# First feed-forward block of an encoder layer: shift rows loaded last, raw first results finished with a bias, and the opening's order set by the scheduler

## What is computed

```python
cc = jax.nn.silu(c)
mod = (cc @ w_ada[l] + b_ada[l]).reshape(b, N_ADA, D_MODEL)
sh1, sc1, gt1, sh2, sc2, gt2, sh3, sc3, gt3 = [mod[:, i, None, :] for i in range(N_ADA)]
h = modulate(rms_norm(x, g_ffn1[l]), sh1, sc1)          # h * (1 + scale) + shift
x = x + 0.5 * gt1 * swiglu(h, w_ffn1_in[l], w_ffn1_out[l])   # a, b = split(h @ w_in); (silu(a) * b) @ w_out
h = modulate(rms_norm(x, g_mix[l]), sh2, sc2)
x = x + gt2 * token_mix(h, ...)                          # chunk attention and pooling, gated
h = modulate(rms_norm(x, g_ffn2[l]), sh3, sc3)
x = x + 0.5 * gt3 * swiglu(h, w_ffn2_in[l], w_ffn2_out[l])
```

## Time and profile before

| | |
|---|---|
| three runs | 1554.09, 1555.72, 1558.91 us (median 1555.72) |
| the profiled execution | 1556.88 us, its span 1555.3 us on core 6 |
| spans of the 8 cores | 1548.9 to 1555.3 us, granted clock 0.987 to 0.997 |
| PE busy | 1497.7 us (96%), 7553 matmuls |
| DVE, ACT, POOL busy | 804.0, 451.8 and 97.7 us |

### The profile page before, as it was taken

One profiled execution on the slowest core, in us unless ns is written; L12 is line 12 of the kernel. 1 busy time (PEld: TensorE's weight loads), 2 busy tenths in 40 slices (PEclk: granted clock), 3 DMA queues, 4 the chain that ended last, 5 costly groups with the idle time before them and its releaser, 6 DMA issues.

```text
span 1555.3 us, 21416 instructions; the slowest of 8 cores (1548.9 to 1555.3 us)
## 1 busy us (share of the span) xinstructions
PE 1497.7 (96%) x7553; PEld 678.1 (44%) x7553; DVE 804.0 (52%) x1262; ACT 451.8 (29%) x581; POOL 97.7 (6%) x210
## 2 busy tenths in 40 slices
PE   2989999999999999999899999999999999999998
PEld 0434444444444444444444444444444444444444
DVE  3567537347336436756863357734544352515316
ACT  6661010110110114666622377423511101010110
POOL 0001000010010000001111011010010001001000
PEclk8999999999999999999999999899999999999999
DMA  9947062171352425024155234244050504105005
GB/s 286 297 141 135 28 136 55 55 141 29 96 114 57 95 86 131 1 42 67 30 82 82 41 55 69 38 72 68 15 81 1 82 1 77 21 6 88 14 1 217
DMA packets 47416, 121.71 MB, mean 78 GB/s; under 512 B 4432, under 2 KB 4560, under 8 KB 47184
## 3 DMA queue, kind: packets, MB, share of 16 engines
q0 software_dynamic: 30176, 57.84, 24.2%
q1 hardware_dynamic: 17136, 62.49, 12.2%
HBM read 169.77 MB, written 8.39 MB: 115 GB/s over the span
## 4 chain that ended last, share of the span: by engine, by line
PE 90%; ACT 3%; DMA 3%; DVE 2%; issue 1%; SPq 1%; ACTq 0%; DVEq 0%; POOLq 0%
PE ps L496 90%; DMA arena<-w_ada 2%; ACT arena L507 2%; SPq L555 1%; DVE arena L525 1%; ACT arena L508 0%; DMA arena<-w_in 0%; DVE arena L526 0%; ACT L508 0%; DVE arena L535 0%; ACT L507 0%; DVE arena L516 0%; DVE arena L548 0%; ACTq L236 0%; DVEq L236 0%
## 5 line engine op out<-in xcount | busy, mean ns | idle before, releaser
L496 PE MATMUL ps<-arena 128*128 128x512 bf16 (+5 forms) x7553 | 1497.7, 361 | 53.7 <-ACT arena L507 27.2
L496 PEld LDWEIGHTS ps<-arena 128*128 128x128 bf16 (+1 forms) x7553 | 678.1, 98 | 872.9 <-issue 124.0
L507 ACT ACTIVATE arena<-ps 128x512 bf16<-128x512 f32 (+3 forms) x344 | 254.3, 760 | 909.8 <-PE ps L496 905.5
L516 DVE TENSOR_TENSOR arena<-arena,ps 128x512 bf16<-128x512 bf16 (+1 forms) x230 | 175.0, 762 | 514.1 <-PE ps L496 495.9
L525 DVE SCALAR_TENSOR_TENSOR arena<-ps,arena 128x512 f32<-128x512 f32 (+1 forms) x410 | 314.5, 773 | 136.0 <-PE ps L496 87.2
L507 ACT ACTIVATE arena<-arena 128x1024 bf16<-128x1024 f32 (+2 forms) x98 | 94.3, 983 | 66.4 <-DVE arena L525 61.4
L516 DVE TENSOR_TENSOR arena<-arena 128x512 bf16<-128x512 bf16 (+10 forms) x183 | 88.0, 506 | 30.6 <-ACT arena L507 26.6
L526 DVE SCALAR_TENSOR_TENSOR arena<-arena 128x1024 f32<-128x1024 f32 x72 | 87.6, 1220 | 18.1 <-DMA arena<-w_ada 17.3
L525 DVE SCALAR_TENSOR_TENSOR arena<-arena 128x512 f32<-128x512 f32 (+2 forms) x115 | 80.2, 722 | 13.7 <-ACT arena L507 12.0
L508 ACT ACTIVATE arena<-arena 128x512 bf16<-128x512 f32 (+2 forms) x88 | 55.2, 645 | 52.1 <-DVE arena L525 41.9
L555 POOL DMA_DIRECT2D arena<-w1i x20 | 13.6, 680 | 441.6 <-PE ps L496 441.6
(11 more groups left out here) (15 smaller groups left out, 44.4 us busy)
## 6 DMA issues: line engine op xcount, KB each, us to landing
arena<-w_ada SPq DMA_DIRECT2D x72, 512.0 KB, 5.3
arena<-w_in POOLq DMA_DIRECT2D x28, 512.0 KB, 6.6
arena<-xT SPq DMA_DIRECT2D x20, 512.0 KB, 13.4
arena<-w3i POOLq DMA_DIRECT2D x20, 512.0 KB, 8.4
arena<-w1i POOLq DMA_DIRECT2D x16, 512.0 KB, 10.0
outT<-arena SPq DMA_DIRECT2D x16, 512.0 KB, 2.7
arena<-w1o POOLq DMA_DIRECT2D x10, 512.0 KB, 16.7
arena<-w3o POOLq DMA_DIRECT2D x10, 512.0 KB, 12.4
```

What stands on the lines that cost most here:

```text
L496: return lambda e: e.matmul(o, lhsT=lhsT, rhs=rhs, start=start, stop=stop)
L507: return lambda e: e.activation(out=o, in_=i, func=func, scale=scale)
L516: return lambda e: e.tensor_tensor(out=o, in0=a, in1=b, op=op)
```

## The change

1. **Loads.** Behind the x of blocks 0 and 1 come only 4 tiles of `w1i` (two hidden tiles) and the 8 *scale* rows; then the other 4 tiles of `w1i`, the x of block 2, the 8 *shift* rows, and the x of blocks 3 and 4. The rows pass through four places (`RING`) in the space of block 3.
2. **Raw results.** H of blocks 0, 1 and 2 is at first made with the scale alone. `FIRST` now holds hidden tiles 0 and 1 of blocks 0 and 1, 64 matmuls; tiles 2 and 3 of both blocks follow. Their results are copied out of PSUM in f32 (`raw_out`: ACT 128x512 and DVE 128x512 for the first two tiles, ACT 128x1024 for the others). Block 2's four units stay in PSUM.
3. **Bias.** Once all shifts are there, 64 matmuls of *one column* multiply the same weights by the shift (`SHB`) into `BIAS`. `biased` finishes each of the 12 units: Silu with a bias on ACT, add and product on DVE (8 of them wholly from SBUF).
4. **H made whole on GpSimd.** Later groups need H with the shift. 17 multiply-adds (`ts` on "pool") do it for blocks 0 and 1 from `XR`, 8 products and 8 multiply-adds for block 2: 33 instructions on POOL, which had none of these.
5. **Order.** The opening up to the last unit of the first group is a zone of its own (zone 1) that is scheduled, with levels and a queue order for SP (`behind`); `order()` now takes any number of zones. The costs of the opening's POOL operations are 1.9. From the first out-projection on, PE, ACT, DVE, POOL and SP run what they ran before, in the same order.
6. The `warm` matmuls are 12, before the first real one, in place of 10 and 7 times 5.

```diff
@@ order @@
-        strict = {e: ([deque(), deque()]) for e in self.ENG}
+        nz = max(r.zone for r in recs) + 1
+        strict = {e: [deque() for _ in range(nz)] for e in self.ENG}
...
-        limit = {"sc": 2, "kq": 2, "pv": 1, "gx": 2, "gy": 1}
-        dma_free = [0.0]
+        limit = {"sc": 2, "kq": 2, "pv": 1, "gx": 2, "gy": 1, "fx": 3}
+        dma_free = [2.5]
...
+            for q in r.nxt:
+                q.need -= 1
+                q.ready = max(q.ready, t + c)
@@ build_nc, the opening @@
-    for i in range(16):
-        slot = RING[i % 6]
-        P.stt(slot, slot, 1.0, CB[:, :], ALU.mult, ALU.mult, accum=RAW[:, i, 0:1])
...
-            for b in range(2):
-                P.act(H[b][:, kt, :], XR[b][:, kt, :], AF.Identity, scale=SCALE[kt], bias=SHIFT[kt])
...
-            if kt < 7:
-                warm(5, 7, False)
+    def row_dot(i, n, sem):
+        slot = RING[i % 4]
+        sp(slot, w_ada[n], sem)
+        with level(-1):
+            P.stt(slot, slot, 1.0, CB[:, :], ALU.mult, ALU.mult, accum=RAW[:, i, 0:1])
+
+    for kt in range(8):
+        row_dot(kt, 8 + kt, "d_a%d" % (kt % 4))
...
+                        P.act(H[b][:, kt, cs], v, AF.Identity, scale=SCALE[kt])
+        for u in range(2):
+            for half in range(2):
+                for b in range(2):
+                    P.mm(FIRST[u][b].one(half), piece(half)[:, u, kt * 128:(kt + 1) * 128], H[b][:, kt, :], kt == 0, kt == 7)
+    for j in range(2):
+        for half in range(2):
+            sp(LATE[2 * j + half], w1i[half * NJ + 2 + j], "d_s%d" % (4 + 2 * j + half))
+    x_load(2)
...
+            if u > 1:
+                P.act(RAWP[u][b], pb.two(), AF.Copy)
+            else:
+                P.act(RAWP[u][b][:, 0, :], pb.one(0), AF.Copy)
+                P.copy(RAWP[u][b][:, 1, :], pb.one(1))
...
+            P.stt(H[2][:, kt, :], xb(2)[:, kt, :], SCALE[kt], r2, ALU.mult, ALU.mult)
...
+    for kt in range(8):
+        row_dot(8 + kt, kt, "d_a%d" % (kt % 4))
...
+                    P.mm(bb[:, n:n + 1], piece(2 * (u // 2) + half)[:, u % 2, kt * 128:(kt + 1) * 128], SHB[:, kt, 0:1],
+                         kt == 0, kt == 7)
...
+            r = P.act(s, pa, AF.Silu, bias=BIAS[:, 2 * u, 0:1])
...
+            P.stt(ACTB[b][:, u, :], pb_, BIAS[:, 2 * u + 1, 0:1], s, ALU.add, ALU.mult)
...
+                        P.ts(H[b][:, kt, cs], v, DER[:, 0, kt:kt + 1], ALU.mult, "pool", DER[:, 1, kt:kt + 1], ALU.add)
+    for kt in range(8):
+        t = T4[kt % 2]
+        P.tt(t, xb(2)[:, kt, :], r2, ALU.mult, "pool")
+        P.ts(H[2][:, kt, :], t, DER[:, 0, kt:kt + 1], ALU.mult, "pool", DER[:, 1, kt:kt + 1], ALU.add)
```

More of the change, by code:

```diff
@@ L810, in build_nc @@
     for b in range(2):
         st, _ = norm_parts(b, 0, "mix")
-        for f in st:
+        with level(1):
+            for f in st:
+                f()
+            for kt, cs, v in XR[b]:
+                P.tt(v, xb(b)[:, kt, cs], RSTD[b][:, cs], ALU.mult)
+    for j in range(2):
+        for half in range(2):
+            cast = P.act(piece(half)[:, j, :], RING[2 * j + half], AF.Copy)
+            if j == 0 and half == 0:
+                wk = pbank().one(0)
+                for _ in range(12):
+                    P.mm(wk, WARM[:, 0:128], WARM[:, :], True, True, cast)
@@ new lines, in build_nc @@
+            P.stt(H[2][:, kt, :], xb(2)[:, kt, :], SCALE[kt], r2, ALU.mult, ALU.mult)
+    third = [pbank(2, "fx") for u in range(4)]
+    for u in range(3):
+        first_mm(third[u], u, 2)
+    for kt in range(8):
+        row_dot(8 + kt, kt, "d_a%d" % (kt % 4))
+        with level(0):
+            P.act(SHIFT[kt], RAW[:, 8 + kt, 0:1], AF.Identity, bias=CST[:, 8 + kt:9 + kt])
+            P.act(SHB[:, kt, 0:1], RAW[:, 8 + kt, 0:1], AF.Identity, bias=CST[:, 8 + kt:9 + kt])
+    bb = pbank().one(0)
@@ L839, in build_nc @@
+    for u in range(3):
+        biased(u, 2, third[u].one(0), third[u].one(1))
     P.copy(DER[:, 0, :], RAW[:, 16:24, 0])
     P.copy(DER[:, 1, :], RAW[:, 24:32, 0])
+    st3, ap3 = norm_parts(3, 0, "act")
+    with level(-1):
+        for f in st3:
+            f()
+    lnexp = P.newest["act"]
+    with level(-1):
+        for f in ap3:
+            f()
+    for u in (1, 2, 3, 0):
+        for b in range(2):
+            biased(u, b, RAWP[u][b][:, 0, :], RAWP[u][b][:, 1, :], lnexp)
+    biased(3, 2, third[3].one(0), third[3].one(1), lnexp)
@@ L841, in build_nc @@
+    st4, ap4 = norm_parts(4, 0, "act", r=RSTD[1])
+    with level(-1):
+        for f in st4:
+            f()
+    with level(0):
+        for f in ap4:
+            f()
     ada_j = [16]
@@ L873, in ffn, with unit @@
         ucnt = [0]
-        def unit(k, jj, b, done=None):
+        def unit(k, jj, b):
             g, c = chunks[k]
@@ L922, in body @@
                 nload[0] = 2
-                for u in range(4):
-                    unit(u // 2, u % 2, blocks[0], done=u)
             else:
                 wi_load()
-            wo_load(0)
+            with level(-1):
+                wo_load(0)
             for bi, b in enumerate(blocks):
-                if bi == 0 and started:
+                if bi < 3 and started:
                     continue
```

256 lines of the change are left out of this document (146 added, 110 removed).

## The result

The changed kernel takes 1568.45 us (median; 1566.79 to 1569.87), the kernel before 1555.72. The ratio is 1.0079, with a 95% interval of 1.0059 to 1.0099: slower by 12 to 13 us, where 1549 and faster had been forecast. The profiled execution took 1566.79 us; its slowest core, core 1, has a span of 1565.2, 9.9 above the 1555.3 of the profiled execution before.

What follows compares the result with a forecast made beforehand. PE, busy 96% of the span, was taken as the bound. An 11 us gain in the opening less 4 for VectorE beside GpSimd gave 7: 1556.9 to 1549.9, with the median 1.2 lower, 1549; range 1540 to 1565.

Steps and rivals of the forecast that it cites:

- E: End of the first 20 out-projections: 172.1 us before; 161 forecast without any further cost.
- step 9: VectorE and GpSimd computing together, 75 to 130 us: lengthening of VectorE unknown, 0 to 45 us, taken as 4.
- step 7: Gate rows behind block 4's x: last six in pairs at 5.5 us per pair, gate at 132, E 161.
- Steps 1 to 3: Opening through block 2 and shifts: first row product 29.9, eighth scale row 41.4, PE start 32.4, shifts to about 72.5.
- Step 4: 64 one-column bias matmuls on PE: 3.1 to 6.3 us, taken as 4.8, PE then at 86.
- Step 5: Block 3: Ln at 86, then 8 products and 8 raw finishes at 0.70 to 0.75 us, to 99.
- Step 6: Block 4: last x load issued 97, landed 102, last column at 117, PE ends the group at 125, not 137.5.
- Step 8: GpSimd's 33 operations from about 75: 1.4 us each for the sum, 1.6 for safety; queue hidden up to 2.1 apiece.
- Rival C: Opening: VectorE and GpSimd exclude each other, gate 25 us later, E 186, time 1565, slower; chance 0.16.
- Rival D: Opening: PE's clock stays low through short waits, at 0.85 E 7 us later, 1556; chance 0.24 together with no-change rival.
- Rival A: Opening: nothing interferes, bias 3.1 us, no idle for columns; E 158 to 161, gain 11 to 14, 1543; chance 0.20.

Runs made afterwards that it cites:

- neither, w1o held: Changed kernel without GpSimd's 33 computing operations or the last eight w_ada rows, its two w1o loads held until block 3's statistics: ratio 0.9935, 1550.48 us.
- six loads late: Changed kernel with GpSimd's queue, from the first weight load for chunk 2 on, held until the gate is computed: ratio 0.9994.
- with finish order 2, 3, 1, 0: Changed kernel with ScalarE shift, early gate rows, new finish order, own places for unit 1's raw results and first four scale rows: 1546.38 us, ratio 0.9931.
- the last versions: Changed kernel with ScalarE shift, early gate rows, new finish order, own raw-result places; first scale rows in own places, 1546.38 us (0.9931), or not, 1546.81 us (0.9933).

## Why the prediction was wrong, step by step

The marker and the moments before it, in us, on the core named; the ratio is against the kernel before.

| kernel | core | Ln, block 3 | last x load, block 4 | first add | marker | ratio |
|---|---|---|---|---|---|---|
| before | 6 | - | 73.9 | 140.0 | 174.7 | 1 |
| changed | 1 | 86.9 | 107.7 | 156.1 | 188.2 | 1.0079 |
| no gate rows | 4 | 86.8 | 108.6 | 139.1 | 174.1 | 0.9995 |
| no GpSimd, w1o held | 1 | 84.2 | 97.3 | 146.1 | 178.4 | 1.0036 |
| neither, w1o held | 4 | 84.7 | 98.5 | 133.7 | 168.8 | 0.9935 |
| six loads late | 6 | 89.4 | 109.0 | 148.7 | 179.2 | 0.9994 |
| ScalarE shift, early gate rows | 2 | 86.9 | 101.3 | 137.0 | 172.5 | 0.9970 |
| with finish order 2, 3, 1, 0 | 3 | 84.8 | 95.8 | 126.8 | 162.3 | 0.9931 |

Set beside each other: the forecast had E at 165 (161 and 4 us of step 9), measured is 185.6. Two terms were too small, the landings in step 7 and the exclusion in step 9.

*Steps 1 to 3, the front*, were nearly right: first row product 31.63 (29.9 forecast; seven of VectorE's squares stand ahead of it until 31.7), eighth 44.40 (41.4), last shift row product 73.28 (72.5). PE's real start was 34.29 (32.4).

*Step 4, the bias*, was costed too high. The 64 one-column matmuls show 2.9 us busy, under the lower end of 3.1, and the bias is copied at 79.75. It decided nothing.

*Step 5, block 3*: Ln at 86.94 (86), right. But then sixteen products, forecast to end at 99, ended at 110.0. The twelve and the four did not take 0.70 to 0.75 us apiece but 1.33 and 1.19 at the mean: this is step 9.

*Step 6, block 4*: last x load 107.7 (97), Ln 119.95 (about 105), and PE ends the group near 138 (125). The chain is as forecast and each delay was passed on whole; its size comes from step 9.

*Step 7, the gate*, failed by itself. Forecast 132, measured 156; of these 24 us some 10 come with step 9 (first add 156.1 to 146.1 without GpSimd's computing), and 14 belong here. The step that failed is the price of 5.5 us for a pair of rows, which leaves about 3 for the landing. Rows 7 don't show 3 us: they show 7.3 at the median, for four loads issued in the stretch in which the kernel before, too, sends the same six weight loads from GpSimd's queue. So the competition stood in the row, and I took the low end of "3 to 7" for loads that I had placed at 113 to 130 with the weight loads at 129 beside them. With 7.3 a pair would have cost 7.3 + 2.4 = 9.7, three pairs 29; that estimate has the gate at 144 and E at 173, no gain even without step 9.

Measured from the end of the second gate row's product to the end of the last one's (on the core of the table): 27.5 us in the changed kernel (landings of 8.5 at the median, waits of 6.67 and 5.42, DMA share 1.05), 28.2 without GpSimd's computing, 17.5, or 5.8 a pair, with the six loads held.

*Step 8, GpSimd*: a multiply-add over 512 from one SBUF input takes 0.73 us alone (twelve in 8.79) and a two-input product 1.26. Forecast 1.4 and 1.6 for each. GpSimd is done at 115 and never late. The estimate by the Trainium skill's page GPSIMD Engine Reference, section Elementwise — side-by-side cycle accounting, 1.1 us for a two-input operation, is about as far below the measured 1.26 as my 1.4 was above it.

*Step 9, VectorE beside GpSimd*, taken at 4 us, cost 6 to 9 at the end. Sixteen of VectorE's instructions with two SBUF inputs met a computing GpSimd and took 20.7 us (15.90 + 4.76) instead of 11.2 at 0.70. The term was mis-sized because I took the value near the end of the only row there was, one in which GpSimd merely issues loads. The Trainium skill's page SBUF — State Buffer, section Who interferes with whom, had the mechanism: two SBUF inputs on VectorE contend with GpSimd's reads of SBUF. The trace agrees: the f32 products take 1719 ns at the mean beside GpSimd and 748 behind it, while the form with a PSUM input stays at 747. That the second waits out one whole instruction, as the forecast had it, is too little for an unbroken row: a product waited out many GpSimd instructions.

*Rival C* gave 1565 and the time was 1568, but not by its mechanism alone. It had GpSimd ending at 145 and 25 us added to the gate. GpSimd ended at 115, the exclusion was worth 6 to 9 us, and the rest was competition for the DMA engines, which no rival named. That its number is near is luck. *Rival D* did not set the end: the low granted clock of 0.73 from 138 to 157 lies where PE waits for the adds anyway, and with the gate rows left out the same stretch has 1.00. From 64 to 138 the clock is 0.88 to 0.89 (0.94 before, rows 2; 0.93 to 0.94 without the gate rows), in a stretch in which PE works 59 of 74 us; no run tried its share alone. *Rival A's* 1543 (E of 158 to 161) is near to what the last versions reach, 1546 with E = 159.7: the opening could be shortened as computed, but not in this order of loads.

## What to carry to other kernels

A step moved to the end of a queue is priced with what will share its transfer engines at its new time: list all queues' issues in that window, and take the landing time from a row with the same company. Work given to an idle GpSimd isn't free while VectorE reads two SBUF operands: give it to ScalarE, as the last versions did, or to a stretch in which VectorE reads one input from PSUM (those instructions kept 0.75 us; a kernel made so wasn't tried). And an experiment that removes work from an in-order queue also releases the loads behind it: pin them where they were, or the run compares two things.

## What the runs showed of the hardware

- VectorE, two SBUF inputs of 128x512 f32, beside a computing GpSimd: 0.75 to 1.75 us apiece and once 3.48, 1.19 to 1.33 at the mean instead of 0.70; GpSimd's own multiply-add 1.52 instead of 0.77, its product 1.69 instead of 1.26. With one PSUM input VectorE is unchanged at 0.75.
- The exclusion is not fair: beside 17 GpSimd instructions in an unbroken row (12.79 us) a VectorE product of 1.22 us ended only behind the row on five of eight cores, 9.9 to 11.7 us; on the other three it took 1.5 to 1.7, and the next pair was held to the row's end, 5.3 to 5.5 us. Where GpSimd alternates two kinds of operation with gaps of 0.18 us, VectorE did get in between. What decides who goes first is open.
- A 512 KB load of SyncE's queue landed in 4.3 us at the median with GpSimd's queue held, in 8.5 with six loads of 512 KB from that queue beside it.
- 64 one-column matmuls show 2.9 us busy in all.
